# A two-block transformer kernel: weight sums made in DRAM by accumulating DMAs instead of by GpSimd and VectorE, and a new order of the first weight splits

## The reference, cut to what matters

```
for l in range(2):
    h = rms_norm(x, g_mix[l]);  proj = h @ w_in[l]
    ... three mixers (softmax attention over 512 tokens), gated and merged ...
    x = x + merged @ w_o[l]
    h = rms_norm(x, g_ffn[l])
    x = x + (silu(h @ w1[l]) * (h @ w3[l])) @ w2[l]      # w1, w3: 1024 x 2816, w2: 2816 x 1024
```

## Time and profile before

| what | us |
|---|---|
| median of 3 runs (lowest, highest) | 3257.82 (3256.49, 3259.09) |
| the profiled execution's own time | 3259.56 |
| its span, first to last instruction | 3257.9 |
| TensorE busy (matmuls) | 3203.1, 98% |
| VectorE busy | 2030.9, 62% |
| ScalarE busy | 1400.4, 43% |
| GpSimd busy | 775.7, 24% |
| mean granted TensorE clock | 0.996 |

### The profile page before, as it was taken

One profiled execution on the slowest core, in us unless ns is written; L12 is line 12 of the kernel. 1 busy time (PEld: TensorE's weight loads), 2 busy tenths in 40 slices (PEclk: granted clock), 3 DMA queues, 4 the chain that ended last, 5 costly groups with the idle time before them and its releaser, 6 DMA issues.

```text
span 3257.9 us, 41235 instructions
## 1 busy us (share of the span) xinstructions
PE 3203.1 (98%) x16588; PEld 2727.8 (84%) x16588; DVE 2030.9 (62%) x2980; ACT 1400.4 (43%) x2175; POOL 775.7 (24%) x562
## 2 busy tenths in 40 slices
PE   9999999999999999999999999999999999999998
PEld 7888888788888888888888888888888898788887
DVE  6865775777848655846949665554544268974433
ACT  5653553344437634633424433332423248843221
POOL 1521241223304311520325022110211013521101
PEclk9999999999999999999999999999999999999999
DMA  4122323232231122222222322222232222223322
GB/s 136 48 74 68 107 94 101 82 110 91 85 115 55 64 72 93 102 97 97 99 90 91 107 81 81 88 84 91 91 103 91 101 85 93 91 91 100 101 97 84
DMA packets 85150, 295.78 MB, mean 91 GB/s; under 512 B 9568, under 2 KB 12128, under 8 KB 84960
## 3 DMA queue, kind: packets, MB, share of 16 engines
q1 hardware_dynamic: 84384, 292.76, 27.0%
q10 hardware_dynamic: 576, 0.40, 0.0%
HBM read 291.02 MB, written 2.10 MB: 90 GB/s over the span
## 4 chain that ended last, share of the span: by engine, by line
PE 78%; DVE 13%; ACT 4%; issue 3%; POOL 2%; DMA 0%; SPq 0%; ACTq 0%; POOLq 0%; DVEq 0%
PE bank L352 77%; DVE wl L670 5%; PE bank L355 2%; ACT wh L611 1%; DVE s_raw L660 1%; ACT m_p L614 1%; DVE small L1427 1%; POOL f_t L714 1%; POOL u_g L714 1%; DVE f_t L660 1%; DVE u_uc L666 0%; DVE m_ptl L670 0%; DVE h_l L673 0%; DMA s_raw<-in_wts 0%; DVE m_qf L660 0%
## 5 line engine op out<-in xcount | busy, mean ns | idle before, releaser
L670 DVE TENSOR_TENSOR wl<-s_raw,wh 128x1024 fp32r<-128x1024 f32 (+1 forms) x563 | 734.1, 1308 | 552.2 <-ACT wh L611 551.1
L352 PE MATMUL bank<-zh,wh 128*128 128x512 f32 (+1 forms) x2588 | 946.9, 366 | 5.7 <-ACT zh L611 5.7
L352 PE MATMUL bank<-zh,wl 128*128 128x512 f32 (+1 forms) x2588 | 942.4, 364 | 5.0 <-DVE wl L670 5.0
L352 PE MATMUL bank<-zl,wh 128*128 128x512 f32 (+1 forms) x2588 | 939.8, 363 | 1.7 <-DVE zl L673 1.6
L611 ACT ACTIVATE wh<-s_raw 128x1024 fp32r<-128x1024 f32 (+1 forms) x563 | 575.1, 1028 | 550.2 <-PE bank L352 410.1
L352 PEld LDWEIGHTS bank<-zh,wl 128*128 128x128 f32 x2588 | 489.1, 189 | 88.7 <-DVE wl L670 11.4
L352 PEld LDWEIGHTS bank<-zh,wh 128*128 128x128 f32 x2588 | 489.6, 189 | 80.2 <-ACT zh L611 5.7
L352 PEld LDWEIGHTS bank<-zl,wh 128*128 128x128 f32 x2588 | 489.3, 189 | 75.8 <-DVE zl L673 3.0
L714 POOL TENSOR_TENSOR f_t<-f_t 128x512 f32<-128x512 f32 x84 | 118.1, 1406 | 524.7 <-DVE f_t L666 524.7
L720 POOL TENSOR_TENSOR small<-small 128x1 f32<-128x1 f32 (+3 forms) x35 | 43.0, 1229 | 822.1 <-DVE small L663 822.1
L352 PE MATMUL bank<-n_h,wh 128*128 128x256 f32 (+1 forms) x448 | 136.9, 306 | 24.9 <-ACT s_s L611 17.6
(11 more groups left out here) (379 smaller groups left out, 5849.8 us busy)
## 6 DMA issues: line engine op xcount, KB each, us to landing
s_raw<-in_wts SPq DMA_DIRECT2D x529, 512.0 KB, 3.3
c_nb<-in_c_bias SPq DMA_DIRECT2D x16, 384.0 KB, 3.1
x<-in_xT SPq DMA_DIRECT2D x8, 256.0 KB, 5.7
out<-x SPq DMA_DIRECT2D x13, 128.0 KB, 1.8
b_mask<-in_b_mask SPq DMA_DIRECT2D x2, 576.0 KB, 3.7
r_d<-in_decay SPq DMA_DIRECT2D x4, 256.0 KB, 2.6
s_raw<-in_wts SPq DMA_DIRECT2D x2, 256.0 KB, 3.7
m_t<-in_mla_tab SPq DMA_DIRECT2D x2, 256.0 KB, 4.6
```

The lines of the kernel that those rows point to most:

```text
L352: return self.e.matmul(out, l, r, start=start, stop=stop, skip_group_check=inside)
L670: return self.e.tensor_tensor(out, src, b32(hi), ALU.subtract)
```

## The change

All 32 units' weight sums (16 in each of two layers) are now made in a DRAM tensor `sums` while the layer's attention runs. GpSimd issues the DMAs: for each unit three copies of the weights (1 MB), then four accumulating DMAs of 256 KB each, which add DRAM to DRAM. They are cut into turns, and one turn is taken at the end of each GpSimd iteration of the first attention stage and the dilated and neighbourhood stages, as long as there are any. Each turn first waits for the DMAs of the turn before. `gpsimd_sums` and VectorE's S4 add are gone. SP now loads a unit's two raw halves by two DMAs each, of weights and of sums, and the two buffers `s_b` (512 KB of sums) and `s_h` (256 KB of weights, new) by one each, after the low parts of the unit before have read them. The second part: in the entry of the units the weight splits up to the first S unit's are placed ahead of the token sums by `upto`, and the first token subtractions are made one unit earlier.

```
 class Sp:
+    def load_s(self, n, slot, side, *unit):
+        m, wts, sums = self.m, self.m.A["wts"], s_sums(self.m, unit)
+        f, l, i = unit
+        self.wait_ge("sa", "S4", *unit)
+        if side == "a":
+            self.e.dma_start(m.raw[slot][:, 0:512], wts[n][:, 0:512])...
+            self.e.dma_start(m.raw[slot][:, 512:1024], sums[:, 1024:1536])...
+            return
+        self.e.dma_start(m.raw[slot][:, 0:512], wts[n][:, 0:512])...
+        self.e.dma_start(m.raw[slot][:, 512:1024], sums[:, 1536:2048])...
+        before = (f, l, i - 1) if KINDS[i - 1] == "S" else (f, 0, FF - 1) if l else None
+        if before:
+            self.wait_ge("wl", self.book.s_at(0, before))
+        else:
+            self.wait_ge("mm", "acc", f, l, 0, 0)
+        self.e.dma_start(m.s_b, sums[:, 0:1024]).then_inc(*self.tell("rawb", *unit, by=16))
+        if before:
+            self.wait_ge("wl", self.book.s_at(2, before))
+        self.e.dma_start(m.s_h, wts[n][:, 512:1024]).then_inc(*self.tell("rawh", *unit, by=16))
 class Dve, low_s:
         elif part == 2:
-            self.lo(wl[:, 0:512], src[:, 1536:2048], wh[:, 0:512]).then_inc(*self.tell("wl", c))
-            self.wait_ge("wl", c)
-            self.wait_ge("pl", "S2", *unit)
-            self.tt(src[:, 1536:2048], src[:, 512:1024], src[:, 1536:2048], ALU.add).then_inc(
-                *self.tell("wl", ("S4",) + unit, ("rel", a)))
+            self.lo(wl[:, 0:512], m.s_h, wh[:, 0:512]).then_inc(*self.tell("wl", c))
-def gpsimd_sums(L, F, i):
...
-    L.tt(L.m.s_b, src[:, 0:1024], src[:, 512:1536], ALU.add).then_inc(*L.tell("pl", "S1", *unit))
-    L.wait_ge("pl", "S1", *unit)
-    L.tt(src[:, 512:1024], L.m.s_b[:, 512:1024], src[:, 0:512], ALU.add).then_inc(*L.tell("pl", "S2", *unit))
+def weight_sums(L, l):
+    book, wts, units = L.book, L.m.A["wts"], s_units()
+    last = None
+    def add(to, x, *key):
+        L.e.dma_start(to, x, accum_op=ALU.add).then_inc(*L.tell("sa", *key, by=16))
...
+    for k in range(len(units) + 3):
+        if k < len(units):
+            unit, s, a, b = of(k)
+            if last:
+                L.wait_ge("sa", *last)
+            L.e.dma_start(s[:, 0:1024], wts[a])...          # "c0"
+            L.e.dma_start(s[:, 1024:1536], wts[a][:, 0:512])...     # "c1"
+            L.e.dma_start(s[:, 1536:2048], wts[b][:, 512:1024])...  # "c2"
+            last = ("c2",) + unit
+            yield
+        if 0 < k <= len(units):
+            unit, s, a, b = of(k - 1)
+            L.wait_ge("sa", *last)
+            add(s[:, 0:512], wts[a][:, 512:1024], "S3", *unit)
+            add(s[:, 512:1024], wts[b][:, 0:512], "S1", *unit)
+            last = ("S1",) + unit
+            yield
+        if 1 < k:
+            L.wait_ge("sa", *last)
+            if k <= len(units) + 1:
+                unit, s, a, b = of(k - 2)
+                add(s[:, 1024:1536], s[:, 512:1024], "S2", *unit)
+                last = ("S2",) + unit
+            if 2 < k:
+                unit, s, a, b = of(k - 3)
+                add(s[:, 1536:2048], s[:, 1024:1536], "S4", *unit)
+                last = ("S4",) + unit
+            yield
+def sum_turn(L):
+    next(L.sums, None)
 gpsimd_mla, gpsimd_dil, gpsimd_nbr, at the end of each iteration:
+        sum_turn(L)
 scalar_ffn1 (vector_ffn1 likewise):
-        for j in TOKEN_SUMS.get(i, ()):
-            scalar_token_sum(L, F, j)
-            L.ahead()
+        if i == 4:
+            upto(L, c - 2)
+            scalar_token_sum(L, F, 0)
+            scalar_token_sum(L, F, 1)
+            upto(L, c - 1)
+            scalar_token_sum(L, F, 2)
+        if i == 5:
+            scalar_token_sum(L, F, 3)
+            upto(L, c)
```

## The result

The changed kernel takes 3645.99 us (median of 4 runs, 3638.76 to 3648.09) against 3258.45 us (4 runs) for the kernel before: a ratio of 1.1185, 95% interval 1.1165 to 1.1204. The profiled execution took 3644.5 us, with a span of 3642.3 us and a mean granted TensorE clock of 0.946. I had forecast 3474 us, in a range of 3235 to 3780.

A forecast was written before the change was run, and what follows sets the result against it. TensorE, busy 98% of the span, was taken as the bound. From 3259.6 us, minus 48 feed-forward gain (34 + 14), plus 264 attention growth, is 3475.6; less 1.7 for the runs' median, 3474 us, range 3235 to 3780.

The forecast's parts named there:

- s_s row: Feed-forward units: TensorE's wait-table row for the stall behind VectorE's S4 sum, 18 stalls, 17.6 us; forecast to be gone.
- T: Attention: one GpSimd turn from issue to landing, taken as 6.0 us, bounds 3.9 and 9.9; 4.8 to 7.5 gives 3360 to 3615.
- the prediction's own formula: Attention growth per layer: 47 T - 150.0 us, or 30 T - 84.3 if more; 132 us a layer, 264 in both.
- The upper bound's picture: GpSimd's DMAs: a copy passes memory twice, an accumulation three times, each issue takes 1.02 us; 9.9 us a turn.
- The stall of the units: Seven-product units: TensorE's 1.14 us stall needing S4 goes in 30 of 32 units, 34 us gained (bounds 17.6 and 43).
- The entry: Entry of the feed-forward units: splits ahead of token sums remove TensorE's waits and slow clock, 14 us gained (bounds 5 and 14).
- The six loads of a unit: Feed-forward units: six DMAs, 1.75 MB against 1 MB, DMA share 0.53, cost nothing.
- The clock: Stretched attention: TensorE at clock 0.50 would make 2.5 us of work 5, under a turn of 6, above 3.9.
- rival 1: Attention: turns cost only what plain loads cost, 3.9 us each; total 3275 us; 20%.
- rival 2: Attention: turn waits are hidden within GpSimd's iterations, only the gain is left, 3210 us; decides below 3.6 us a turn; 12%.
- Rival 3: Attention: accumulating DMAs are slow, turns near 10 us or above; at 9.9 the total is 3840 us; 8%.
- rival 4: Feed-forward units: the stall stays, units stay at 11.2 us, only the 14 us are won, total 3508 us; 5%.

The follow-up runs named there:

- experiment 1: Changed kernel without its turns: GpSimd issues no DMA, SP loads weights in place of sums, so weight sums are left out; 3219.55 us.
- experiment 8: Kernel of experiment 1 with the old order of token sums and weight splits (second part of the change left out); 3228.33 us.
- experiment 7: Kernel before with only the second part of the change, the new order of splits and token sums; 3255.5 us, ratio 0.9992.
- experiment 2: Changed kernel with each accumulating DMA made a plain copy of the same size and place; 3468.96 us (one run).
- experiment 4: Changed kernel with three semaphores: a turn waits only for the turn it reads from and the third turn before it; 3351.07 us.
- experiment 9: Kernel of experiment 6 without turns in the neighbourhood stage: 8 in the output projection, the last 7 behind GpSimd's first feed-forward units; 3240.68 us, ratio 0.9951.
- experiment 3: Changed kernel with every GpSimd DMA cut to 64 columns (32 KB) and SP loading weights in place of sums; 3331.27 us (one run).
- experiment 5: Changed kernel with the same turns and waits spread further apart, through attention and the output projection; 3279.24 us, ratio 1.0062.
- experiment 6: Experiments 4 and 5 together: turns spread out, with three semaphores; 3268.44 us, ratio 1.0028.
- experiment 10: As experiment 9, but two turns in each of the output projection's 8 iterations and none beside the feed-forward units; 3266.29 us, ratio 1.0025.

## Why the prediction was right, and where its sizes were off

The mechanism, its place and its sign were as forecast: GpSimd's turn waits, the divisions stand behind it, TensorE behind these, and the feed-forward part gains less than attention loses. The wait rows, units of 10.02 us (10.1 forecast), and the vanished s_s row all came. Not every mark of it came: TensorE was to be busy for under half of the first attention stage and is busy for 62%, since its matmuls take longer at the lower clock (142.78 us for the 542 in that window, 81.31 for 461 before), and the stage takes 224 us, not 180. The size is well off: the change was to cost 216 us and costs 388, and T is above the 4.8 to 7.5 of the forecast's own inner band. That 3646 lies in the range is owed to its upper end, which was set for T = 9.3. The time is 172 us above 3474, by these terms.

**The turn's length** was the mis-sized term: T = 6.0 was taken, 7.61 was measured. Put into the prediction's own formula, 47 x 7.61 - 150.0 is 208 us a layer, 415 in both; the ledger has 419.5. This T is the distance of the turns in the same trace, so the agreement says that the divisions keep the turns' pace, and not much more; with the 7.25 and 7.09 us from issue to landing, which is how the prediction defined T, the formula gives 374. The 0.3 us from a landing to the next turn's start, 47 times in a layer, are most of what is then missing. For the other kernels it comes out low by about 20 us. Over experiment 1, plain copies (T = 5.66) give 2 x (47 x 5.66 - 150.0) = 232 where 249 were measured, and tiny DMAs (T = 4.16) give 2 x (47 x 4.16 - 150.0) = 91 where 112 were. So what failed is only the price of a turn, "a third of the way up" between 3.9 and 9.9; three fifths would have hit. Low was the price of the accumulating pass: 177 us of the growth go away with plain copies. The upper bound's picture, two reads and one write, was nearer than I credited. The issue was priced too high there, at 1.02 us: a copy's takes 0.53 to 0.79 us and an accumulation's 0.8 to 1.2, about 5.1 us for the seven of a unit in place of 7.1.

**The stall of the units** was to give 34 us and gives 30 (experiment 8). **The entry** was to give 14 us and gives 9 with the sums gone and 3 by itself (experiments 8 and 7). I took the upper bound of 14, on the argument that the sums' removal frees VectorE at the same place. That help is there (6 us come only with both), but part of the stall stays as waits of about 1 us, and the old layer-0 stall of 5.29 us had already fallen to 2.03 with the sums gone, since it was in part VectorE slowed beside GpSimd's sum (experiment 8). Together 48 forecast, 39 to 40 measured.

**The six loads of a unit cost nothing**, as said: a DMA share of 0.57 where I had 0.53, and the units keep 10.02 us.

**The clock** did drop in the stretched attention, to 0.74 and 0.73. The prediction named this as what could upset the sum. It didn't: 94 of 96 turns start 0.29 us after a landing, so the landings and not TensorE set the pace.

**The rivals.** Rivals 1 and 2 needed a T of 3.9 or less. That isn't reached even by 32 KB DMAs, whose turns stand 4.16 us apart (though they land in 3.5). Rival 3 (T near 10) is above the measured value, and rival 4 fell with the units' 10.02 us. The Trainium skill, page "DMA: Bandwidth & Descriptors", section "Anatomy of one DMA — SWDGE (gpsimd) path", gives about 2.1 us for 32 KB, 2.6 for 256 KB and 3.2 for 512 KB. The traces agree for 32 KB (2.2 us copied or accumulated from the weights, 2.7 accumulated within the sums), but not for the DRAM to DRAM transfers of size: 4.0 to 4.4 for 256 KB copied, 5.3 to 5.6 accumulated, 4.6 for 512 KB. These have others of their turn in flight beside them; the four copies of 256 KB that are alone in their turn (experiment 2) took 3.7 to 4.8 us, so company isn't the reason.

What stays open: experiment 4 parts the wait from the DMA engines' time only for that placement, and about 19 us of experiment 9 in attention are not broken down further. The weight loads of attention do land later there (4.5 us on the mean against 3.6 in experiment 1) and ScalarE waits longer for them (94.4 against 74.4 us); that this makes the 19 us is argued, not shown. Whether a turn beside each seven-product unit is free was not run.

## What to carry to other kernels

A DMA issued by an engine that also computes costs that engine the issue, and, if its next DMA waits for the last one, the landing too. Multiply that by the loop's iterations before moving "free" work to DMA, and compare one turn with one iteration. The same 49 turns a layer cost 426 us, 131, 60 or 21 us by depth and place alone: spread them to where the issuing engine is idle and the DMA share is low enough, keep them off the head of a stage, and add up the queue's own time against the stretch that it is put in. And measure an unfamiliar DMA form by itself before trusting bounds from plain loads.

## What the runs showed of the hardware

- The seven DMAs of a unit cost the 16 DMA engines 1.6 times as much when four of them accumulate as when all copy: 390 us of all engines' time against 243 for the same 67.12 MB. Half of the bytes are accumulated, so if the copied half takes the same 122 us in both, the accumulated half takes 268, about 2.2 times a copy (an estimate from these two runs).
- Full DMA engines slow both queues: at a DMA share of 1.00 GpSimd's 256 KB DMAs land in 9 us instead of 5.5, with three turns in flight, and SP's weight loads of 512 KB in 8.5 instead of 3.4 (experiment 4 over 67 to 290 us, experiment 1 over 67 to 215).
- A VectorE subtraction of 128x512 took 2.89 us beside a GpSimd add of 128x1024, and 0.68 without it (kernel before and experiment 8).
- The span ends 7.5 us after VectorE's last instruction in the profiled execution of the changed kernel, and 2.5 us after it in the kernel before. It is the 5 us that the ledger leaves over. The trace has it in a drain at GpSimd's end, which the other engines' last instructions wait for; here in the changed kernel, then in experiment 4 (min, median and longest in ns, first and last start in us):

```profile
L4326 POOLq DRAIN  x1: 10094/10094/10094, 3632.0 to 3632.0; - x1
```
```profile
L4344 POOLq DRAIN  x1: 3266/3266/3266, 3340.2 to 3340.2; - x1
```

It takes 10.1 to 11.7 us in the four kernels whose 224 DMAs of GpSimd tell one semaphore (the changed one, experiments 2, 3 and 5), 3.3 us in the four where the same DMAs tell three (4, 6, 9, 10), and 2.6 us in the four without such DMAs. No run tells whether the number of semaphores or the depth of the waits makes the difference.
